# Reordered PSUM reads, split steps and the last up and down products in the MLPs of a two-layer trunk kernel

## What is computed

```
def squared_relu_mlp(h, w1, w2):        # h (512, 1024), w1 (1024, 4096), w2 (4096, 1024)
    return jnp.square(jax.nn.relu(h @ w1)) @ w2
...
for i in range(DEPTH):                  # DEPTH = 2
...
    x = x + squared_relu_mlp(rmsnorm(x, norm_ffn_g[i]), ffn_w1[i], ffn_w2[i])
```

## Time and profile before

| | |
|---|---|
| median of 3 runs | 1170.44 us (1170.16 to 1172.05) |
| the profiled execution, own time | 1171.35 us |
| its span, first to last instruction | 1169.3 us |
| mean granted TensorE clock | 0.993 |
| PE busy | 1140.8 us, 98% |
| PE weight loads busy | 1003.9 us, 86% |
| DVE busy | 829.2 us, 71% |
| ACT busy | 635.7 us, 54% |
| POOL busy | 251.3 us, 21% |
| PE's share of the chain of waits that ended last | 82% |

### The profile page before, as it was taken

One profiled execution on the slowest core, in us unless ns is written; L12 is line 12 of the kernel. 1 busy time (PEld: TensorE's weight loads), 2 busy tenths in 40 slices (PEclk: granted clock), 3 DMA queues, 4 the chain that ended last, 5 costly groups with the idle time before them and its releaser, 6 DMA issues.

```text
span 1169.3 us, 16188 instructions
## 1 busy us (share of the span) xinstructions
PE 1140.8 (98%) x6556; PEld 1003.9 (86%) x6556; DVE 829.2 (71%) x933; ACT 635.7 (54%) x773; POOL 251.3 (21%) x211
## 2 busy tenths in 40 slices
PE   8999999999999999999999999999989999999997
PEld 6888888989999999788888888888989999999975
DVE  7787647677786786777487656655757678677778
ACT  7664434765555655545444432543576656556555
POOL 0040035113012121113164044004511211112020
PEclk9999999999999999999999999999999999999999
DMA  9523134969789777735232622313587977977673
GB/s 349 206 80 101 55 135 107 244 133 192 196 181 201 186 143 164 174 73 198 91 97 84 216 91 72 108 36 144 118 227 158 198 191 179 207 171 154 146 133 102
DMA packets 48457, 176.59 MB, mean 151 GB/s; under 512 B 5504, under 2 KB 5632, under 8 KB 47744
## 3 DMA queue, kind: packets, MB, share of 16 engines
q0 software_dynamic: 18432, 67.12, 31.9%
q1 hardware_dynamic: 28368, 104.35, 26.5%
q10 hardware_dynamic: 1584, 4.10, 1.0%
HBM read 173.45 MB, written 2.10 MB: 150 GB/s over the span
## 4 chain that ended last, share of the span: by engine, by line
PE 82%; DVE 9%; DMA 3%; ACT 3%; issue 2%; POOL 0%; SPq 0%; DVEq 0%; ACTq 0%; POOLq 0%
PE psum L1874 11%; PE psum L1876 11%; PE psum L1875 11%; PE psum L2149 8%; PE psum L2150 8%; PE psum L2151 8%; PE psum L2129 8%; PE psum L2131 7%; PE psum L2130 7%; DVE w_lo L1181 2%; DMA w_raw<-in_up 2%; DMA w_raw<-in_weights 1%; DVE w_lo L1170 1%; PE psum L2066 1%; ACT w_hi L725 1%
## 5 line engine op out<-in xcount | busy, mean ns | idle before, releaser
L1181 DVE TENSOR_TENSOR w_lo<-w_sum,w_hi 128x1024 fp32r<-128x1024 f32 x112 | 136.5, 1223 | 84.2 <-ACT w_hi L725 83.9
L2149 PE MATMUL psum<-w_lo,slot_hi 128*128 128x512 f32 x448 | 176.3, 394 | 5.2 <-DVE y_rows L1519 5.2
L2150 PE MATMUL psum<-w_hi,slot_hi 128*128 128x512 f32 x448 | 176.3, 393 | 0.0
L2151 PE MATMUL psum<-w_hi,slot_lo 128*128 128x512 f32 x448 | 175.6, 392 | 0.0
L725 ACT ACTIVATE w_hi<-w_sum 128x1024 fp32r<-128x1024 f32 x112 | 117.7, 1054 | 79.8 <-PE psum L2151 76.0
L2129 PE MATMUL psum<-xs_s_lo,w_hi 128*128 128x256 f32 x512 | 145.4, 284 | 0.9 <-DVE a L1457 0.8
L2131 PE MATMUL psum<-xs_s_hi,w_lo 128*128 128x256 f32 x512 | 144.9, 283 | 0.0
L2130 PE MATMUL psum<-xs_s_hi,w_hi 128*128 128x256 f32 x512 | 144.8, 283 | 0.0
L1827 POOL DMA_DIRECT2D w_sum<-in_down x64 | 55.4, 866 | 373.5 <-DVE w_lo L1181 373.5
L1181 DVE TENSOR_TENSOR w_lo<-w_raw,w_hi 128x1024 fp32r<-128x1024 f32 x80 | 101.0, 1265 | 48.7 <-ACT w_hi L725 48.4
L725 ACT ACTIVATE w_hi<-w_raw 128x1024 fp32r<-128x1024 f32 x80 | 83.9, 1056 | 80.0 <-PE psum L2131 64.1
(11 more groups left out here) (226 smaller groups left out, 2701.1 us busy)
## 6 DMA issues: line engine op xcount, KB each, us to landing
w_raw<-in_weights SPq DMA_DIRECT2D x90, 512.0 KB, 3.7
w_sum<-in_down POOLq DMA_DIRECT2D x64, 512.0 KB, 6.9
w_sum<-in_down SPq DMA_DIRECT2D x48, 512.0 KB, 4.5
w_raw<-in_up POOLq DMA_DIRECT2D x48, 512.0 KB, 6.4
w_raw<-in_up SPq DMA_DIRECT2D x32, 512.0 KB, 3.9
up<-in_up SPq DMA_DIRECT2D x16, 512.0 KB, 4.3
up<-in_up POOLq DMA_DIRECT2D x16, 512.0 KB, 7.2
x<-in_x_t SPq DMA_DIRECT2D x2, 1024.0 KB, 8.8
```

What stands on the lines that cost most here:

```text
L1181: dve.tensor_tensor(w_lo[:, c % RING, :], buffer(kind, SUM_BUFFER[STAGE[p][0]] + half), w_hi[:, c % RING, :].bitcast(F32), ALU.subtract).t ...
L2149: pe.matmul(to, s_hi[:, k, tok], w_lo[:, c % RING, cols], start=first, stop=False, skip_group_check=True)
L2150: pe.matmul(to, s_hi[:, k, tok], w_hi[:, c % RING, cols], start=False, stop=False, skip_group_check=True)
L2151: last = pe.matmul(to, s_lo[:, k, tok], w_hi[:, c % RING, cols], start=False, stop=(kp == 1 and j == 1), skip_group_check=True)
```

## The change

Three things are changed, in both layers, and in `mlp_steps` and the lists of all five engines.

1. The up products of block 0: on DVE c11 moves ahead of one weight split, the halves of c12 and of c22 each ahead of the split that stood ahead of them; on ACT the squares of c12's and c22's results move behind one or two splits.
2. On SP, at the start, the reload for U1P2 and the load for D0P3 move behind the reload for U1P1.
3. From U3P3 on, the order becomes U3P6, D2P6, U3P7, U3P4, D2P7, D2P4 and then D3 as before, where it was D2P6, U3P6, D2P7, U3P7, D2P4, U3P4. The loop of every engine breaks off at c == FB - 1, and a list of its own follows; c22 of block 3 is done in halves, the sums s1 to s4 of block 3 move up beside D2P7 and D2P4.

```diff
+LAST_UPS = (("D", "P1"), ("U", "P1"), ("D", "P2"), ("U", "P2"), ("D", "P5"), ("U", "P5"), ("D", "P3"), ("U", "P3"),
+            ("U", "P6"), ("D", "P6"), ("U", "P7"), ("U", "P4"), ("D", "P7"), ("D", "P4"))
...
-    for b in range(FB - 1):
+    for b in range(FB - 2):
         for p in ORDER:
             steps += [("D", b, p, h) for h in range(2)] + [("U", b + 1, p, h) for h in range(2)]
+    steps += [(kind, FB - 2 + (kind == "U"), p, h) for kind, p in LAST_UPS for h in range(2)]
```

On SP:

```diff
-                refill(l, "U", 0, "P2")
-                sp.wait_ge(lo_ready, N.lo[f"xs{l}", "P4"] + 1)
-                for name in ("11", "22"):
-                    for half in range(2):
-                        quarter(l, "D", 0, name, half)
+                sp.wait_ge(lo_ready, N.lo[f"xs{l}", "P4"] + 1)
+                for half in range(2):
+                    quarter(l, "D", 0, "11", half)
+                refill(l, "U", 0, "P4")
+                refill(l, "U", 0, "P2")
+                for half in range(2):
+                    quarter(l, "D", 0, "22", half)
                 refill(l, "U", 0, "P7")
-                refill(l, "U", 0, "P4")
```

On ACT, first at the start:

```diff
                 ahead("U", 0, "P7", 0)
+                ahead("U", 0, "P7", 1)
                 squared(0, 1, a12, "P6")
-                ahead("U", 0, "P7", 1)
+                ahead("U", 0, "P4", 0)
                 operand(0, "P2", a12, h=1)
-                ahead("U", 0, "P4", 0)
+                ahead("U", 0, "P4", 1)
                 squared(0, 2, a22, "P7")
-                ahead("U", 0, "P4", 1)
```

and behind the loop, with b = 2 and c = 3:

```diff
+                ahead("U", c, "P6", 0)
+                keep_p3(c)
+                ahead("U", c, "P6", 1)
+                ahead("D", b, "P6", 0)
+                ahead("D", b, "P6", 1)
+                squared(c, 1, a12, "P6")
+                ahead("U", c, "P7", 0)
+                operand(c, "P1", a11, h=0)
+                ahead("U", c, "P7", 1)
+                ahead("U", c, "P4", 0)
+                squared(c, 2, a22, "P7")
+                ahead("U", c, "P4", 1)
+                ahead("D", b, "P7", 0)
+                last_quarter(c)
+                ahead("D", b, "P7", 1)
+                ahead("D", b, "P4", 0)
+                operand(c, "P2", a12, h=1)
+                ahead("D", b, "P4", 1)
                 b = FB - 1
-                last_quarter(b)
                 ahead("D", b, "P1", 0)
                 operand(b, "P5", s1, summed=1)
```

On DVE, first at the start:

```diff
+                c11(0)
                 ahead("U", 0, "P5", 0)
-                c11(0)
...
-                ahead("U", 0, "P6", 1)
                 dve.wait_ge(ssq_step, SUMMED[norm])
                 c12(0, half=0)
+                ahead("U", 0, "P6", 1)
+                c12(0, half=1)
                 ahead("U", 0, "P7", 0)
-                c12(0, half=1)
                 row_scales()
+                c22(0, half=0)
                 ahead("U", 0, "P7", 1)
-                c22(0, half=0)
+                c22(0, half=1)
+                ahead("U", 0, "P4", 0)
                 operand(0, "P2", a12)
-                ahead("U", 0, "P4", 0)
-                c22(0, half=1)
                 ahead("U", 0, "P4", 1)
```

and behind the loop, with b = 2 and c = 3:

```diff
+                ahead("U", c, "P6", 0)
+                ahead("U", c, "P6", 1)
+                c12(c)
+                ahead("D", b, "P6", 0)
+                ahead("D", b, "P6", 1)
+                ahead("U", c, "P7", 0)
+                read(b, "P6")
+                operand(c, "P1", a11)
+                c22(c, half=0)
+                ahead("U", c, "P7", 1)
+                c22(c, half=1)
+                ahead("U", c, "P4", 0)
+                ahead("U", c, "P4", 1)
+                ahead("D", b, "P7", 0)
+                sum_s1(c)
+                ahead("D", b, "P7", 1)
+                sum_s3(c)
+                sum_s2(c)
+                ahead("D", b, "P4", 0)
+                read(b, "P7")
+                operand(c, "P2", a12)
+                ahead("D", b, "P4", 1)
+                sum_s4(c)
                 b = FB - 1
-                sum_s1(b)
                 ahead("D", b, "P1", 0)
-                sum_s3(b)
                 operand(b, "P5", s1)
+                read(b - 1, "P4")
                 ahead("D", b, "P1", 1)
-                sum_s2(b)
-                sum_s4(b)
+                operand(b, "P3", a12)
                 ahead("D", b, "P2", 0)
-                operand(b, "P3", a12)
                 read(b, "P1")
```

POOL issues the adds of U3P6 ahead of those of D2P6. On PE, behind the loop:

```diff
+                kept_done(c, "P1")
+                up_product(c, "P6")
+                read_done(b, "P1")
+                down_product(b, "P6")
+                sum_done(c, "P6")
+                up_product(c, "P7")
+                pe.wait_ge(sum_half, 3 * l + 3)
+                up(c, "P4", 0)
+                sum_done(c, "P7")
+                up(c, "P4", 1)
+                read_done(b, "P6")
+                down_product(b, "P7")
+                read_done(b, "P7")
+                down_product(b, "P4")
                 b = FB - 1
                 read_done(b - 1, "P4")
                 down_product(b, "P1", fresh=True)
```

More of the change, by code:

```diff
@@ L998, in mlp @@
                     ahead("U", c, "P3", 1)
+                    if c == FB - 1:
+                        break
                     ahead("D", b, "P6", 0)
@@ L1835, in mlp @@
                     for p in ("P1", "P5", "P3", "P6"):
+                        if (b, p) == (FB - 2, "P6"):
+                            add_quarters(l, "U", b + 1, p)
+                            add_quarters(l, "D", b, p)
+                            continue
                         add_quarters(l, "D", b, p)
@@ L2214, in mlp @@
                 sums(f"stat_ffn{l}", ST, norm=norm)
-                pe.wait_ge(sum_half, 2 * l + 1)
+                pe.wait_ge(sum_half, 3 * l + 1)
                 up(0, "P7", 0)
@@ L2219, in mlp @@
                 wait_split((f"xs{l}", "P4"))
-                pe.wait_ge(sum_half, 2 * l + 2)
+                pe.wait_ge(sum_half, 3 * l + 2)
                 up(0, "P4", 0)
```

## The result

The changed kernel takes 1182.99 us (median of 4 runs, 1182.64 to 1184.92) against 1171.14 us of before beside it: 11.85 us more, ratio 1.0108 with a 95% interval of 1.0092 to 1.0124. The forecast was 1181.3, with a range of 1173 to 1189. The profiled execution has a span of 1180.8 us and a mean granted clock of 0.988, where before had 1169.3 and 0.993.

A forecast was written before the change was run, and what follows sets the result against it. PE's own pace bounds the kernel, so only its idle time and the clock after it count. Ends lose 10.7 us per layer, 21.4, less 10.5 gained at the starts: 10.9 more, 1181.3 us, range 1173 to 1189.

The forecast's parts named there:

- The start: Block 0's up products, both layers: shorter transposes' wait, no waits at U0P7 and U0P4, full clock; 10.5 us less.
- D3P1 behind D2P4: End of each MLP: D3P1 waits 5.15 us for the read of P4, behind a split and an operand on DVE.
- The order alone: At D3P1: DVE's list order makes the 5.15 us wait, with no other work having to be late.
- D2P4 behind D2P7: End of each MLP: D2P4 waits 6.2 us for the read of P7, DVE being late through D3P1's first load.
- floor 4.0: At D2P4: wait of 4.0 us from DVE's list order only, if DVE is not late.
- The clock: After each new wait at D2P4 and D3P1 the granted clock falls, costing 1.7 us each.
- D3P3's old wait and clock: End of each layer: D3P3's wait of 2.6 us and its slow clock of 1.7 us go, 4.3 us gained.
- The upper bound of 1188 us: Top of the forecast's own bounds, 1174 to 1188 us, reached by half of the heavier case.
- the heavier case: Rival at the end: first load 1.2 us later per layer, each clock fall 3.4 us; 1191 us, 8%.
- The rivals: Four alternatives: both ends gain, 6%; waits at floor without second clock fall, 6%; heavier, 8%; start gives only c11, 5%.
- No read came at once: Rival at the end: reads of P7 and P4 come at once, so both ends gain; 1158 us, 6%.
- the clock fell at all four waits: Against the rival with waits at D2P4 and D3P1 at their floor and no clock fall; 1170 us, 6%.

The follow-up runs named there:

- P7's read first: Changed kernel, with only DVE's read of P7 moved to right behind the split of D3P1's first half; 1174.7 us, ratio 1.0042 to before.
- P4's read first: Changed kernel, with only DVE's read of P4 moved ahead of the split of D3P5's first half; 1176.8 us, ratio 1.0057 to before.
- the end alone: Changed kernel with the start's edits taken back, so only the end's order differs from the kernel before; 1193.3 us, ratio 1.0212.
- both reads first: Changed kernel, with DVE's reads of P7 and P4 both moved ahead of splits at the end; 1165.6 us, ratio 0.9971 to before.
- P2 first: Kernel with the start's edits and U3P4 between D2P7 and D2P4, block 3's down products now beginning with P2's first half; 1164.3 us, ratio 0.9958 to before.
- the start alone: Kernel before with only the start's edits of SP, ACT and DVE, end unchanged; 1158.1 us, ratio 0.990; again 1158.6 us, ratio 0.9896.

## Why the prediction was right, and where its terms were off

**The start** (forecast -10.5): -11.05 in the trace, -11.3 alone. The steps were the right ones: 1.13 us at the transposes, both waits at U0P7 and U0P4 gone, U0P4 at full clock. The difference is almost 0.6 us: a wait of 0.3 us at U0P7 in the other layer, below what the waits' view lists, and in the layer with the counted wait 0.3 us more than the 0.8 of the view. SP's part at nothing was shown by undoing it.

**D3P1 behind D2P4** (5.15): 5.02 in both layers. "The order alone" was right while D2P4 waits; the run with P7's read first shows that the add DMA stands close behind it.

**D2P4 behind D2P7** (6.2, floor 4.0): 5.49 and 5.56. The chain was followed step by step, and only the load was clearly mis-sized. The split of D2P4's first half ended at 464.00 and w_hi of D3P1 started at 467.44, 3.4 us later where I took 3.9; so the load holds up the split behind s1 by 0.2 us instead of 0.7. The rest of the difference is the same list, a little tighter than my pitches. In the run with P4's read first ACT waited up to 3.0 us for the two pieces, and D2P4 up to 7.5: the load is a term with a spread of its own. The fit of the Trainium skill ("DMA: Bandwidth & Descriptors", "Anatomy of one DMA"), which is for a DMA of GpSimd's path, gives an estimate of 3.2 us for 512 KB. This load, of SP, landed 3.3 us after its issue, nearer to that than to the row's median of 3.9; but the same loads took 4.2 to 6.0 us in the run with P4's read first, so one load doesn't bear the estimate out.

**The clock** (1.7 us for each of four waits, 6.8, less 3.4 of before): this is the term that was mis-sized. Measured 2.79, 2.98, 3.00 and 1.47, together 10.2. That is 3.4 us too little in the forecast. Against it stand 1.35 us too much at D2P4, 0.55 too little gained at the start, 0.3 too much at D3P1 and 0.3 too little for D3P3's old wait and clock. So 10.9 becomes 11.9, and that the forecast came within 1 us of it is in part luck: errors of opposite sign. Nor is 10.2 a fixed number: over all 16 waits of 5.0 us and more in these profiles the cost was 2.3 us on average, and the end alone lost 8.1 us at its four. The prediction's own words on the clock were a little strong: 5.15 us is about twice 2.6, not over twice.

**The bounds.** The upper bound of 1188 us doesn't follow from the sum given for it: half of the heavier case's 9.2 us on 1181.3 is 1185.9. Nothing hangs on it, as the measured time lies below both.

**The rivals.** None came true. No read came at once, the clock fell at all four waits, and the heavier case's 3.4 us per fall was not reached.

## What to carry to other kernels

Where an engine that works in order holds both a read that lets TensorE go on and a preparation for a step further on, the read goes first, above all where the preparation waits for the same product. Here PE waited 4.9 to 5.4 us at each of the two places in the changed kernel and 1.9 to 2.6 with both reads first, and one such exchange elsewhere, in both layers, was worth 3.4 us by itself. Two products on one accumulator need another product between them: with U3P4 between D2P7 and D2P4 the wait at D2P4 was gone, and moving that product out for the sake of a later wait had moved the cover away. When a wait of a few us is taken away, look which DMA it had covered: with P7's read first, and with P2 first, part of what was gained went to loads and adds of 512 KB.

## What was not expected of the hardware

The clock after a wait of PE. Over the profiles of the study, counting waits within the MLPs' down products from start to start: after the two of 1.5 us it stayed; after 19 between 1.9 and 3.1 us it fell 11 times, at a cost of 1.5 to 1.7 us each time; after 16 of 5.0 to 7.7 us it fell every time, at 1.5 to 3.0 us. Waits of equal length went both ways (2.67 us: 1.67 lost in the kernel before, less than 0.1 with the start alone), and seven waits of 5.02 us cost anything from 1.5 to 3.0. So the same wait can bring two numbers 1.6 us apart per layer. The runs of one kernel lie 0.8 to 7.4 us apart; that the clock makes this spread is not shown, as only one execution of each was profiled. One pattern is in the counts: six of the 19 waits ended at most 10 us after an earlier wait of PE had ended, and the clock fell after all six; of the other 13 it fell after five. What decides between them was not tried.

The adds of POOL, 512 KB each, landed after 5.2 to 12.2 us in the kernel before, with a median of 6.7, and after 8.3 at the critical place of the run with P7's read first. SP's plain loads of the MLPs' weights had a median of 4.3 us, from 3.1 to 14.4. In the median a piece that is built by adding in place needs 2.4 us more lead than one that is loaded. With one step less of it (P2 first) ACT waited for it again and again.
